# Feeding the last gated FFN of the first block: raw columns for three pairs, normalised columns for nineteen

## The reference, cut to what matters

```python
h = layer_norm(ALPHA * h + mix, ln2_g[l], ln2_b[l])
h = layer_norm(ALPHA * h + 0.5 * swiglu(h, ffn2_w_gate[l], ffn2_w_up[l], ffn2_w_down[l]),
               ln3_g[l], ln3_b[l])
...
def swiglu(x, w_gate, w_up, w_down):
    return (jax.nn.silu(x @ w_gate) * (x @ w_up)) @ w_down
```

## Time and profile before

| | |
|---|---|
| median of three executions | 1949.44 us (1946.74 to 1949.81) |
| profiled execution, first to last instruction (span) | 1945.9 us; what lies around it is not recorded, the median of the runs is 3.5 us above |
| TensorE busy | 1931.2 us, 99% of the span |
| VectorE, ScalarE, GpSimd busy | 74%, 52%, 8% |
| granted TensorE clock, mean | 0.999 |

### The profile page before, as it was taken

The page is one execution under the profiler, slowest core; times in us unless marked ns, Lnnn a source line. Parts: engine busy times, 40 slices in busy tenths (PEclk is TensorE's granted clock), DMA queues, the critical chain, the costliest instruction groups (busy, mean ns, idle before and its releaser), DMA issues.

```text
span 1945.9 us, 42335 instructions
## 1 busy us (share of the span) xinstructions
PE 1931.2 (99%) x16150; PEld 1892.7 (97%) x16150; DVE 1431.5 (74%) x2591; ACT 1019.8 (52%) x1527; POOL 152.7 (8%) x192
## 2 busy tenths in 40 slices
PE   9999999999999999999999999999999999999998
PEld 8999989999999999899999999999999999999998
DVE  6774787987588768879978874667765775667763
ACT  4443687554455447865547443665445444565443
POOL 0001123000100011320010100000000000100000
PEclk9999999999999999999999999999999999999999
DMA  7454433545454544345553665445555555435554
GB/s 265 172 197 170 166 109 112 192 174 193 156 192 172 196 164 145 109 152 194 201 191 140 235 233 183 151 149 185 193 214 177 195 202 208 152 131 195 194 213 154
DMA packets 46830, 346.66 MB, mean 178 GB/s; under 512 B 5344, under 2 KB 6416, under 8 KB 9232
## 3 DMA queue, kind: packets, MB, share of 16 engines
q1 hardware_dynamic: 44416, 335.63, 48.0%
q0 software_dynamic: 2320, 9.74, 1.6%
HBM read 344.29 MB, written 1.07 MB: 177 GB/s over the span
## 4 chain that ended last, share of the span: by engine, by line
PE 91%; DVE 4%; ACT 2%; DVEq 1%; issue 1%; DMA 0%; ACTq 0%; SPq 0%; POOL 0%
PE ps L622 22%; PE ps L623 22%; PE ps L624 22%; PE ps L639 14%; PE ps L630 2%; PE ps L631 2%; PE ps L632 2%; DVE w_lo L1996 1%; PE ps L1162 0%; DVE pj L2465 0%; DMA h<-in_hidden 0%; DVE cst L2486 0%; PE ps L1197 0%; DVE pj L2462 0%; ACT scratch L1669 0%
## 5 line engine op out<-in xcount | busy, mean ns | idle before, releaser
L1996 DVE TENSOR_TENSOR w_lo<-raw,w_hi 128x1024 fp32r<-128x1024 f32 (+1 forms) x582 | 749.3, 1313 | 151.1 <-ACT w_hi L1300 91.5
L622 PE MATMUL ps<-x_hi,w_lo 128*128 128x256 f32 (+3 forms) x2208 | 622.1, 282 | 1.5 <-DVE x_lo L2087 0.6
L624 PE MATMUL ps<-x_hi,w_hi 128*128 128x256 f32 (+3 forms) x2208 | 615.1, 279 | 0.0
L623 PE MATMUL ps<-x_lo,w_hi 128*128 128x256 f32 (+3 forms) x2208 | 614.8, 278 | 0.0
L1297 ACT ACTIVATE w_hi<-raw 128x1024 fp32r<-128x1024 f32 x454 | 466.3, 1052 | 92.5 <-PE ps L639 49.0
L622 PE MATMUL ps<-hid_hi,w_lo 128*128 128x256 f32 (+1 forms) x1536 | 431.5, 281 | 0.1
L624 PE MATMUL ps<-hid_hi,w_hi 128*128 128x256 f32 (+1 forms) x1536 | 430.2, 280 | 0.0
L623 PE MATMUL ps<-hid_lo,w_hi 128*128 128x256 f32 (+1 forms) x1536 | 429.8, 280 | 0.0
L622 PEld LDWEIGHTS ps<-x_hi,w_lo 128*128 128x128 f32 x2208 | 414.9, 188 | 6.4 <-issue 4.2
L623 PEld LDWEIGHTS ps<-x_lo,w_hi 128*128 128x128 f32 x2208 | 415.0, 188 | 0.5
L624 PEld LDWEIGHTS ps<-x_hi,w_hi 128*128 128x128 f32 x2208 | 414.6, 188 | 0.0
(11 more groups left out here) (351 smaller groups left out, 2315.3 us busy)
## 6 DMA issues: line engine op xcount, KB each, us to landing
raw<-in_w_up SPq DMA_DIRECT2D x176, 1024.0 KB, 4.8
raw<-in_w_down SPq DMA_DIRECT2D x64, 1408.0 KB, 6.0
raw<-in_w_in SPq DMA_DIRECT2D x36, 1024.0 KB, 4.8
raw<-in_w_out SPq DMA_DIRECT2D x16, 1024.0 KB, 4.8
cst<-row_copy POOLq DMA_DIRECT2D x2, 1088.0 KB, 8.5
raw<-in_w_up SPq DMA_DIRECT2D x4, 512.0 KB, 7.2
cst<-in_consts POOLq DMA_DIRECT2D x1, 1537.5 KB, 6.5
prm<-in_prm POOLq DMA_DIRECT2D x2, 690.0 KB, 7.2
```

The costliest lines, as they stand in the source:

```text
L622: mm(dst, low, xa, start=first, stop=False)
L623: mm(dst, high, xb, start=False, stop=False)
L624: return mm(dst, high, xa, start=False, stop=last)
L1996: v.tensor_tensor(dst, src, high.bitcast(F32), ALU.subtract).then_inc(lo_done, 1)
```

## The change

In layer 1 the last FFN gets streams of its own, `normed_up` on PE, ACT and DVE, and `normalise` on POOL; all other stages keep theirs.

- PE: pairs 0 to 2 run on the plain operand as before (now all at the tight address). Pair 3 starts the normalised operand: for every chunk it waits for `ln2_low`, and before the first for both units of its weights. Pairs 3 to 21 have 256 columns and use `three`.
- POOL, behind its sums: adds minus mean to chunks 4 to 7 of h in place, waits for DVE's centring of chunks 0 to 3 and for rstd, then multiplies all 8 chunks by rstd in place.
- DVE: in `level_norm` it centres chunks 0 to 3 before it computes the variance. For pairs 0 to 2 it reads both banks out in one go (`evict`), multiplies both by rstd (`scale`), and makes the product and the low part as before; between them lie the weight splits, written out, and the low parts of the 8 chunks of the normalised operand (`chunk`). From pair 3 on the product is read straight from PSUM, and high and low part are both made on DVE (`direct`).
- ACT: per chunk two Identity passes with gain and bias (the high part of the operand, and h itself in place); from pair 3 on Silu straight from PSUM. Its casts of pairs 3 to 21 go away.
- Down projection: `level_down` leaves out the three DVE operations per chunk that normalised h.

The diff, cut to its core:

```diff
+        PLAIN_PAIRS, VECTOR_CENTRES = 3, 4
...
+            def normed_up(q, turn0, norm, T):
+                N, xs = T + 4, (plain_hi, plain_lo_of(LEVEL_NORM[norm]))
+                pe.wait_ge(up_free, q * NF + (CREDIT - 1))
+                first_pair(turn0, LEVEL_NORM[norm], 0, N, xs, {5: lambda: mean(norm, T)}, ready=plain_ready)
+                for f in range(1, PLAIN_PAIRS):
+                    pe.wait_ge(up_free, q * NF + f + (CREDIT - 1))
+                    for u in range(2):
+                        narrow_unit(turn0 + f // 2, f % 2, u, ps[:, 2 * (f % 2) + u, 0:N], N, xs,
+                                    {0: lambda: level_variance(norm, T)} if (f, u) == (1, 0) else {})
+                pe.wait_ge(up_free, q * NF + PLAIN_PAIRS + (CREDIT - 1))
+                first_pair(turn0 + 1, 0, 2, T, None, ready=ln2_low, j=1)
+                with pe.Fori(2, UP_T) as it:
+                    for j in range(2):
+                        pe.wait_ge(up_free, q * NF + it * 2 + (j - 1 + CREDIT))
+                        for u in range(2):
+                            narrow_unit(turn0 + it, j, u, ps[:, 2 * j + u, 0:T], T)
...
+                def gate(f):
+                    j = f % 2
+                    act.wait_ge(gate_ready, q * NF + f + 1)
+                    fn(silu[:, j, 0:T], silu[:, j, 0:T], ACT.Silu, bias=offset(2 * j, T)).then_inc(silu_done, 1)
+                def cast(f):
+                    act.wait_ge(prod_ready, level * NF + f + 1)
+                    fn(hid_of(T)[0][:, f:f + 1, 0:T], prod[:, f % 2:f % 2 + 1, 0:T], ACT.Copy, scale=0.5).then_inc(cast_done, 1)
+                def chunk(k):
+                    act.wait_ge(ln2_scaled, k + 1)
+                    c = h[:, k, T1 - T:T1]
+                    fn(x_of(T)[0][:, k, 0:T], c, ACT.Identity, scale=par(P1, "ln2g", k), bias=par(P1, "ln2b", k))
+                    fn(c, c, ACT.Identity, scale=par(P1, "ln2g", k), bias=par(P1, "ln2b", k)).then_inc(ln2_high, 1)
+                def direct(it, j):
+                    act.wait_ge(unit_used, turn0 * 4 + it * 4 + (2 * j + 1 + START))
+                    fn(silu[:, j, 0:T], ps[:, 2 * j, 0:T], ACT.Silu).then_inc(silu_done, 1)
+                def turn(it, next_width):
+                    for j in range(2):
+                        split_next(turn0 + it, j, W_NARROW if j == 0 else next_width)
+                        direct(it, j)
+                weights(4)
+                gate(0)
+                weights(5)
+                chunk(0)
+                cast(0)
+                chunk(1)
+                weights(6)
+                gate(1)
+                chunk(2)
+                chunk(3)
+                weights(7)
+                cast(1)
+                for k in range(4, KD):
+                    chunk(k)
+                weights(8)
+                gate(2)
+                weights(9)
+                cast(2)
+                direct(1, 1)
+                with act.Fori(2, UP_T - 1) as it:
+                    turn(it, W_NARROW)
+                turn(UP_T - 1, W_WIDE)
...
+                    if gains:
+                        v.tensor_tensor(c, c, neg_mean[:, 0:T], ALU.add)
+                        dve.drain()
+                        v.scalar_tensor_tensor(out=c, in0=c, scalar=gains[:, m:m + 1], in1=rstd[:, 0:T],
+                                               op0=ALU.mult, op1=ALU.mult)
+                        dve.drain()
+                        v.tensor_scalar(c, c, offsets[:, m:m + 1], ALPHA, ALU.add, ALU.mult)
...
+                for k in range(centres):
+                    c = h[:, k, T1 - T:T1]
+                    last = v.tensor_tensor(c, c, neg_mean[:, 0:T], ALU.add)
+                    if k == centres - 1:
+                        last.then_inc(centred, 1)
...
+                def columns(block, n):
+                    v.tensor_reduce(wsum[:, 2 * n:2 * n + 2], block[:, T:T + 4].rearrange("p (h c) -> p c h", h=2), AX_X, ALU.add)
+                def evict(f):
+                    j = f % 2
+                    gate, upb, act_in, half = banks(j)
+                    dve.wait_ge(unit_used, turn0 * 4 + 2 * f + (2 + START))
+                    columns(gate, 2 * j)
+                    columns(upb, 2 * j + 1)
+                    dve.drain()
+                    v.scalar_tensor_tensor(out=act_in, in0=neg_mean[:, 0:T], scalar=wsum[:, 4 * j + 1:4 * j + 2],
+                                           in1=gate[:, 0:T], op0=ALU.mult, op1=ALU.add)
+                    v.scalar_tensor_tensor(out=half, in0=neg_mean[:, 0:T], scalar=wsum[:, 4 * j + 3:4 * j + 4],
+                                           in1=upb[:, 0:T], op0=ALU.mult, op1=ALU.add).then_inc(up_free, 1)
+                def scale(f):
+                    gate, upb, act_in, half = banks(f % 2)
+                    dve.drain()
+                    v.tensor_tensor(act_in, act_in, rstd[:, 0:T], ALU.mult).then_inc(gate_ready, 1)
+                    v.tensor_tensor(half, half, rstd[:, 0:T], ALU.mult)
+                def product(f):
+                    j = f % 2
+                    gate, upb, act_in, half = banks(j)
+                    dve.drain()
+                    dve.wait_ge(silu_done, q * NF + f + 1)
+                    v.scalar_tensor_tensor(out=half, in0=half, scalar=offset(2 * j + 1, T), in1=act_in,
+                                           op0=ALU.add, op1=ALU.mult).then_inc(prod_ready, 1)
+                def product_low(f):
+                    dve.wait_ge(cast_done, level * NF + f + 1)
+                    v.scalar_tensor_tensor(out=hb[:, f:f + 1, 0:T], in0=prod[:, f % 2:f % 2 + 1, 0:T], scalar=0.5,
+                                           in1=ha[:, f:f + 1, 0:T].bitcast(F32), op0=ALU.mult, op1=ALU.subtract)\
+                        .then_inc(hid_ready, 1)
+                def chunk(k):
+                    xa, xb = x_of(T)
+                    dve.wait_ge(ln2_high, k + 1)
+                    v.tensor_tensor(xb[:, k, 0:T], h[:, k, T1 - T:T1], xa[:, k, 0:T].bitcast(F32), ALU.subtract).then_inc(ln2_low, 1)
+                def weights(unit):
+                    lo_next(turn0 * 4 + unit)
+                def direct(it, j):
+                    gate, upb, act_in, half = banks(j)
+                    dve.wait_ge(unit_used, turn0 * 4 + it * 4 + (2 * j + 2 + START))
+                    dve.wait_ge(silu_done, q * NF + it * 2 + (j + 1))
+                    v.scalar_tensor_tensor(out=half, in0=upb[:, 0:T], scalar=0.5, in1=act_in,
+                                           op0=ALU.mult, op1=ALU.mult).then_inc(up_free, 1)
+                    f = it * 2 + j
+                    f = slice(f, f + 1) if isinstance(f, int) else bass.ds(f, 1)
+                    src = prod[:, j:j + 1, 0:T]
+                    dve.drain()
+                    v.tensor_copy(ha[:, f, 0:T], src)
+                    dve.drain()
+                    v.tensor_tensor(hb[:, f, 0:T], src, ha[:, f, 0:T].bitcast(F32), ALU.subtract).then_inc(hid_ready, 1)
+                def turn(it, next_width):
+                    for j in range(2):
+                        split_next(turn0 + it, j, W_NARROW if j == 0 else next_width)
+                        direct(it, j)
+                evict(0)
+                scale(0)
+                weights(4)
+                product(0)
+                weights(5)
+                chunk(0)
+                product_low(0)
+                evict(1)
+                scale(1)
+                chunk(1)
+                weights(6)
+                product(1)
+                chunk(2)
+                chunk(3)
+                weights(7)
+                product_low(1)
+                for k in range(4, KD):
+                    chunk(k)
+                evict(2)
+                scale(2)
+                weights(8)
+                product(2)
+                weights(9)
+                product_low(2)
+                dve.nop().then_inc(gate_ready, UP_PAIRS - PLAIN_PAIRS)
+                direct(1, 1)
+                with dve.Fori(2, UP_T - 1) as it:
+                    turn(it, W_NARROW)
+                turn(UP_T - 1, W_WIDE)
...
+            def normalise(norm, T):
+                pool.wait_ge(neg_ready, norm + 1)
+                pool.wait_ge(plain_ready, LEVEL_NORM[norm] * KD + KD)
+                for k in range(VECTOR_CENTRES, KD):
+                    nc.gpsimd.tensor_tensor(h[:, k, T1 - T:T1], h[:, k, T1 - T:T1], neg_mean[:, 0:T], ALU.add)
+                pool.wait_ge(centred, 1)
+                pool.wait_ge(std_ready, norm + 1)
+                for k in range(KD):
+                    if k == VECTOR_CENTRES:
+                        pool.drain()
+                    nc.gpsimd.tensor_tensor(h[:, k, T1 - T:T1], h[:, k, T1 - T:T1], rstd[:, 0:T], ALU.mult).then_inc(ln2_scaled, 1)
```

(6 more changed lines are left out.)

48 lines of the change are left out of this document (32 added, 16 removed).

## The result

The changed kernel took 1952.34 us (median of 16 executions, 1950.78 to 1955.38), the kernel before, beside it on the same chip, 1949.14 us (16 executions). The ratio is 1.0021, with a 95% interval of 1.0015 to 1.0027: 4.1 us longer, 2.9 to 5.3.

The account below looks back on a forecast made before the run. PE, with a matmul in flight for 99% of the span, was taken to bound the kernel. Gaps and restarts of 10.3 us less 5.0 and 0.85 gave 4.4 us on 1949.44, so 1953.8 us; range 1947.5 to 1959.5.

Parts of the forecast that it names:

- The sum: Whole kernel: gaps 10.0 us, 10.3 with restarts, less 5.0 and 0.85, making it 4.4 us longer.
- The spacing: Up projection, pairs 3 to 21: matmuls go from 118.6 to 113.0 ns each, saving 5.0 us.
- The down projection: Three DVE operations per chunk go, so PE waits less in the crossing behind it, saving 0.85 us.
- Pair 2: Up projection: its weight split comes late, so PE starts at 866.3 in place of 862.09, a 4.2 us gap.
- Pair 3: Up projection: PE is through with pair 2 at 872.1 but goes on at 876.8, a 4.7 us gap.
- Pair 4: Up projection: PE finishes pair 3 at 882.2 but the split comes at 883.2, a 1.1 us gap.
- POOL: DVE's chain up to pair 4: eight places held up beside POOL's operations, about 0.5 us each, 4.5 us in all.
- The price by the whole instruction: Upper bound: each of eight DVE places held up for POOL's full 0.94 us, 3.5 us more, 1957.3 us.
- POOL did not fit into the holes: Rival: POOL's operations fall where DVE reads PSUM or waits, the 4.5 us vanish, 1949.4 us; a tenth and a half.
- the splits did not come in time: Rival: splits for pairs 2 and 3 come in time, no gap, 5.0 + 0.85 stays, 1943.6 us; one tenth.
- the spacing fell: Rival said it would not: 118.6 ns came from where the weights lie, only gaps stay, 1958.8 us; some 0.05.
- The clock's rival: PE's clock falls to 1.2 GHz in the gaps, 2.7 us each: 1956.5 for one, 1959.2 for two; two tenths.

Follow-up runs that it names:

- the kernel without normalising: The changed kernel without any normalising of the residual in this block, pairs 3 to 21 taking an old operand of the same shape; 0.9979 of the kernel before.
- PE kept busy: The changed kernel with nine extra 256-column matmuls ahead of PE's wait for pair 2 and nine ahead of that for pair 3; 1.0019 of the kernel before.
- other order: The change with six pairs on the uncentred operand, all sixteen normalising operations on POOL, early splits, passes spread over pairs 1 to 5; 0.9974 of the kernel before.

## Why the prediction was right

The forecast was 1953.8 us, 4.4 over the median shown; measured are 4.1 (2.9 to 5.3). The mechanism held: the starts of pairs 2 and 3 hang on DVE's and ACT's chain, and they came within 0.3 us of the forecast. One of its own signs of being wrong came all the same, a clock under 1.00 between 860 and 885 (it was 0.50), and the second gap was 2.67 us where 4 to 5 were to be right. The sum put the clock at nothing; that it fits so closely is in part luck, as the falls cost 0.5 us in one execution and 1.8 in another. Its steps, in its order:

- **The spacing**: 113.0 ns forecast, 112.9 measured; 5.0 us forecast, 5.2 in the kernel without normalising. Right.
- **The down projection**: 0.85 forecast for the crossing, 0.80 measured in the changed kernel. DVE adds the last result at 1041.03, 0.04 us behind PE's last matmul there, in place of 1.1, and its centrings come 0.90 earlier. By itself, in the kernel before, it gave 0.49. The wait that gave it back is another than the one named: the 1.2 us without work are two waits of 0.62, at 1050.57 and at 1060.54, and it is the first that went. The first in the kernel before, then in the changed kernel the same matmul and the second wait:

```profile
1050.57 0.36 PE L622 MATMUL ps<-x_hi,w_lo 128*128 128x256 f32 x1 [0.62 <-DVE x_lo L2087]
```

```profile
1054.08 0.29 PE L627 MATMUL ps<-x_hi,w_lo 128*128 128x256 f32 x1
...
1063.96 0.36 PE L627 MATMUL ps<-x_hi,w_lo 128*128 128x256 f32 x1 [0.59 <-DVE w_lo L2075]
```

- **Pair 2**: variance 3.1 us later forecast, 3.2 measured. Pair 2 forecast at 866.3, 17.0 us behind pair 0; measured 17.16. Right, with the holding up of 0.5 us at each place: the centrings, the scaling and the splits show it one by one.
- **Pair 3**: forecast at 876.8, 27.5 us behind pair 0; measured 27.74. The start was right and the hole was not: 4.7 forecast, 2.67 measured. The step that failed is "PE ... is through with pair 2 at 866.3 + 5.8": pair 2 took 7.9 us from its start to its last matmul, as its first 22 ran at half clock. With PE kept busy pair 3 starts 4.78 us after PE could have (871.16 to 875.94).
- **Pair 4**: 1.1 us forecast, none measured; pair 3 at half clock filled it. With PE kept busy it is 1.03.
- **The sum**: the up projection 10.3 - 5.0 = 5.3 us longer forecast; 5.57 and 6.81 measured in two executions, 5.05 with PE kept busy and the clock at 1.00. From pair 0 to the end the two executions are 4.6 and 5.8 us over before, with 4.4 forecast.
- **POOL**: 4.5 us of holding up forecast; 4.9 on DVE's rows, and 4.9 by leaving POOL out, which also takes one fall of the clock away. Of the Trainium skill's rule (SBUF — State Buffer, Who interferes with whom) the runs bear out the kind: DVE's operations with both operands in SBUF were held up, while its read-outs, with one operand in PSUM, stayed at 0.48 us. The price by the whole instruction, 1957.3, was too high: the largest step seen on one DVE operation in the change is 0.54 us (1.22 to 1.76). That bound was also misread: the earlier trace rows have a POOL operation of 1.16 us beside those of 0.94.
- **The rivals**: POOL did not fit into the holes, the splits did not come in time, the spacing fell. The clock's rival was given two tenths as a case beside the forecast, and it came true together with it: two falls in each of the two profiled executions of the change. What did not come true is its price, 2.7 us for each on top; it was 0.5 to 1.8 for both, because the time that PE lost at half speed it would mostly have spent waiting. The Trainium skill (TensorE: Matmul & The Clock Gate, Part 1) has the idle TensorE fall to half rate; the trace agrees, with 0.50 behind both holes.

## What to carry to other kernels

Where one engine bounds the kernel and another feeds it, follow the feeder's chain from its latest input to the first thing that the bound engine needs, and put new operations behind that or spread them out: the change and its other order, which does both, lie 8.6 us apart from pair 0 on. An idle engine is no free help if its operations and a busy engine's shut each other out: count what it holds up (here 0.5 us for most of DVE's operations that met one of POOL's, where one more operation on DVE takes 0.35). A slow clock behind a hole cost here only what the next wait did not swallow (0.5 and 1.8 of some 4 us): fill the hole with work that nobody needs, and see what comes back.
